# Recurrent layer and cross-attention: gates, scans and first scores set among earlier products

## The reference

```python
def rglru_scan(xc, w_a, b_a, w_x, b_x, lam, reverse):     # 16 blocks of 128 columns, two directions
    r = sigmoid(einsum('bshc,hce->bshe', xb, w_a) + b_a)
    i = sigmoid(einsum('bshc,hce->bshe', xb, w_x) + b_x)
    log_a = -RG_LRU_C * r * softplus(-lam)
    a = exp(log_a)
    u = sqrt(-expm1(2.0 * log_a)) * (i * xb)
    return scan of h = a * h + u along the 512 tokens

def rglru_layer(x, ...):
    h = rms_norm(x, norm_g)
    xr, gate = jnp.split(h @ w_in, 2, axis=-1)             # 2048 columns each
    xc = causal convolution of xr over 4 tokens
    y = rglru_scan(xc, ..., reverse=False) + rglru_scan(xc, ..., reverse=True)
    return x + (y * silu(gate)) @ w_out

# second block: mixer, then
x = x + merged @ w_out
def cross_attention(hn, memn, wq, wkv, wo):                # 256 memory rows, 4 heads of 256
    q = (hn @ wq).reshape(b, s, XA_HEADS, XA_DH)
    k, v = split(memn @ wkv)
    p = softmax(einsum('bshd,bmhd->bhsm', q, k) * XA_DH ** -0.5)
    return einsum('bhsm,bmhd->bshd', p, v).reshape(b, s, D_MODEL) @ wo
```

## Time and profile before

| | |
|---|---|
| median of 3 runs | 2404.89 us (2400.52 to 2405.05) |
| the profiled execution | 2402.92 us, of which the span is 2401.1 us |
| PE busy | 2277.0 us, 95% |
| PEld busy | 1807.1 us, 75% |
| DVE busy | 1503.6 us, 63% |
| ACT busy | 1269.8 us, 53% |
| POOL busy | 290.5 us, 12% |
| mean granted clock of PE | 0.98 |

### The profile page before, as it was taken

The page is one execution under the profiler, slowest core; times in us unless marked ns, Lnnn a source line. Parts: engine busy times, 40 slices in busy tenths (PEclk is TensorE's granted clock), DMA queues, the critical chain, the costliest instruction groups (busy, mean ns, idle before and its releaser), DMA issues. The chain is left out here.

```text
span 2401.1 us, 29505 instructions
## 1 busy us (share of the span) xinstructions
PE 2277.0 (95%) x11266; PEld 1807.1 (75%) x11266; DVE 1503.6 (63%) x1863; ACT 1269.8 (53%) x1677; POOL 290.5 (12%) x273
## 2 busy tenths in 40 slices
PE   7999899999998999999999999999996999999994
PEld 6878558877667768998888878888765777777773
DVE  4435742549996677666434545355237999888886
ACT  4334541468883445652324423225324988888884
POOL 2000000023330212240000000000000222212210
PEclk9999999999999999999999999999997999999997
DMA  7122103422224333001322312334224999999994
GB/s 238 62 70 90 51 1 111 129 88 88 88 66 162 129 111 119 19 1 36 105 88 88 106 36 72 127 117 158 71 81 168 400 409 411 407 401 402 399 401 184
DMA packets 119815, 377.39 MB, mean 157 GB/s; under 512 B 9608, under 2 KB 38592, under 8 KB 94496
## 3 DMA queue, kind: packets, MB, share of 16 engines
q1 hardware_dynamic: 106432, 332.49, 37.4%
q0 software_dynamic: 12768, 37.13, 4.7%
q10 hardware_dynamic: 512, 6.34, 0.7%
HBM read 363.02 MB, written 21.02 MB: 160 GB/s over the span
## 5 line engine op out<-in xcount | busy, mean ns | idle before, releaser
L2215 DVE TENSOR_TENSOR w_lo<-raw,w_hi 128x2048 fp32r<-128x2048 f32 x118 | 270.3, 2290 | 490.5 <-ACT w_hi L1570 490.4
L1570 ACT ACTIVATE w_hi<-raw 128x2048 fp32r<-128x2048 f32 x118 | 225.8, 1914 | 434.9 <-PE bank L848 385.8
L848 PE MATMUL bank<-hT_hi,w_hi 128*128 128x512 f32 x512 | 200.3, 391 | 3.7 <-DVE y_lo L2767 2.3
L848 PE MATMUL bank<-hT_lo,w_hi 128*128 128x512 f32 x512 | 199.7, 390 | 0.0
L848 PE MATMUL bank<-hT_hi,w_lo 128*128 128x512 f32 x512 | 199.7, 390 | 0.0
L1057 PE MATMUL bank<-hT_hi,w_hi 128*128 128x512 f32 x448 | 179.6, 401 | 1.8 <-DVE hT_lo L2279 1.8
L1057 PE MATMUL bank<-hT_hi,w_lo 128*128 128x512 f32 x448 | 174.6, 390 | 0.0
L1057 PE MATMUL bank<-hT_lo,w_hi 128*128 128x512 f32 x448 | 174.6, 390 | 0.0
L3006 DVE TENSOR_TENSOR e_lo<-eraw,e_hi 128x2048 fp32r<-128x2048 f32 x62 | 141.9, 2289 | 33.4 <-ACT e_hi L2102 33.4
L2890 DVE TENSOR_TENSOR e_lo<-raw,e_hi 128x2048 fp32r<-128x2048 f32 x64 | 146.4, 2288 | 12.0 <-ACT e_hi L2084 11.7
L2890 DVE TENSOR_TENSOR w_lo<-raw,w_hi 128x2048 fp32r<-128x2048 f32 x64 | 144.7, 2287 | 7.9 <-ACT w_hi L2084 7.6
(11 more groups left out here) (573 smaller groups left out, 5390.4 us busy)
## 6 DMA issues: line engine op xcount, KB each, us to landing
raw<-expert_w_gate SPq DMA_DIRECT2D x64, 1024.0 KB, 11.3
raw<-expert_w_up SPq DMA_DIRECT2D x64, 1024.0 KB, 11.6
eraw<-expert_w_down SPq DMA_DIRECT2D x64, 1024.0 KB, 10.7
raw<-w_in SPq DMA_DIRECT2D x40, 1024.0 KB, 5.1
raw<-even_w_in SPq DMA_DIRECT2D x18, 1024.0 KB, 5.2
raw<-odd_w_in SPq DMA_DIRECT2D x16, 1024.0 KB, 5.4
raw<-even_w_out SPq DMA_DIRECT2D x8, 1024.0 KB, 5.1
raw<-odd_w_out SPq DMA_DIRECT2D x8, 1024.0 KB, 5.1
```

Source lines behind the costliest of these rows:

```text
L848: mm = pe.matmul(out, st, mv, start=first and x == 0, stop=last and x == 2)
L1570: act.activation(w_hi[m % SPL][:], raw[n % RAW][:], ACT.Copy).then_inc(sem("hi_done"), 1)
L2215: dve.tensor_tensor(w_lo[m % SPL][:], raw[split_of[m] % RAW][:], f32(w_hi[m % SPL][:]), ALU.subtract).then_inc(sem("lo_done"), 1)
```

## The change

**Recurrent layer.** The gate products of the blocks 4s - 2 to 4s + 1 now stand behind the four tall panels of stage s (blocks 0 and 1 in stage 0), so only the groups 14 and 15 are left among the units of the output product. ACT's sigmoids, tables and silu, and DVE's `floors` and `recurrence`, have block numbers two higher at the same places of the stage, and fewer of them stand behind the last stage. There, `rnn_hi(0)` is followed by `gate_silu(7)`, and the splits of weights stand in other places.

The diff, with the context cut:

```diff
--- before.py
+++ after.py
@@ -1073,8 +1073,8 @@
                 tall((pn["xr"], pn["r_gate"])[q // 2][2 * s + q % 2], as_it_comes if s == 0 and q == 0 else hT)
-                if s:
-                    gates(4 * (s - 1) + q)
+                if s or q >= 2:
+                    gates(4 * s + q - 2)
         stage(wait=False)
@@ -1102,11 +1102,9 @@
 
-        gates(12)
         rnn_unit(0, 0)
-        gates(13)
+        gates(14)
         rnn_unit(0, 1)
-        gates(14)
         gates(15)
@@ -1367,8 +1365,10 @@
             return mg_hi[:, k], mg_lo[:, k]
-        gemm(pn["mix_out"], merged_in, False)
-        stage(wait=False)
+        gemm(pn["mix_out"][0:1], merged_in, False)
+        stage(wait=False)
+        banks_free(pn["mix_out"][1])
+        gemm_unit(pn["mix_out"][1], 0, merged_in, False)
         last = panels[pn["mix_out"][0]]
@@ -1377,19 +1377,22 @@
                     tr.then_inc(sem("norm_T"), 1)
+        gemm_unit(pn["mix_out"][1], 1, merged_in, False)
         pe.wait_ge(sem("norm_lo"), feat_at["mem"] + KD)
 ...
         gemm(pn["xv"], memT, False)
-        last = panels[pn["xv"][-1]]
-        pe.wait_ge(sem("evac_act"), last["at"] + last["nj"])
-        norm("x")
-        gemm(pn["xq"], hT_as_it_comes("x"), True)
-        stage(wait=False)
-        last = panels[pn["xq"][-1]]
-        pe.wait_ge(sem("evac_act"), last["at"] + last["nj"])
+        for half in range(2):
+            last = panels[pn["xv"][half]]
+            pe.wait_ge(sem("evac_act"), last["at"] + last["nj"])
+            for t in range(NT):
+                turn("x", t, range(4 * half, 4 * half + 4))
+        as_it_comes = hT_as_it_comes("x")
+        gemm(pn["xq"][0:1], as_it_comes, True)
+        banks_free(pn["xq"][1])
+        gemm_unit(pn["xq"][1], 0, hT, True)
         n_x = XH * NT
@@ -1397,7 +1400,7 @@
             for c in range(2):
-                mm = pe.matmul(psum[i % 4][:, 0:MEM], xqT[:, 2 * h + c, t * P:t * P + P], xkT[:, 2 * h + c],
+                mm = pe.matmul(psum[4 + i % 4][:, 0:MEM], xqT[:, 2 * h + c, t * P:t * P + P], xkT[:, 2 * h + c],
                                start=c == 0, stop=c == 1)
@@ -1407,26 +1410,45 @@
                 for m in range(MEM // P):
-                    mm = pe.matmul(psum[6 + c][:], xv[:, m, h * XD + c * P:h * XD + c * P + P], xpT[h % 2][:, m],
+                    mm = pe.matmul(psum[2 + c][:], xv[:, m, h * XD + c * P:h * XD + c * P + P], xpT[h % 2][:, m],
                                    start=m == 0, stop=m == MEM // P - 1)
 ...
 
+        heads_there = set()
+
+        def attended(k):
+            if k not in heads_there:
+                heads_there.add(k)
+                pe.wait_ge(*after("xa_lo", k + 1))
+            return xo_hi[:, k], xo_lo[:, k]
+
+        last = panels[pn["xq"][0]]
+        pe.wait_ge(sem("evac_act"), last["at"] + last["nj"])
         for i in range(3):
             xscores(i)
+        gemm_unit(pn["xq"][1], 1, hT, True)
+        stage(wait=False)
         for i in range(n_x):
 ...
                 xscores(i + 3)
+            if i == 0:
+                last = panels[pn["xq"][1]]
+                pe.wait_ge(sem("evac_act"), last["at"] + last["nj"])
             pe.wait_ge(*after("xa_norm", i + 1))
 ...
             for m in range(MEM // P):
-                tr = pe.transpose(psum[4 + i % 2][:, m * P:m * P + P], xprobs[i % 4][:, m * P:m * P + P], ident)
+                tr = pe.transpose(psum[i % 2][:, m * P:m * P + P], xprobs[i % 4][:, m * P:m * P + P], ident)
             tr.then_inc(sem("xa_tr"), 1)
 ...
                 xattend(i // NT - 1)
+            for j in {n_x - 3: (0, 1), n_x - 2: (2,), n_x - 1: (3,)}.get(i, ()):
+                pe.wait_ge(*after("xa_exp", n_x - 3 + j))
+                gemm_unit(pn["xo"][0], 0, attended, False, js=(j,))
         xattend(XH - 1)
-        stage()
-        gemm(pn["xo"], lambda k: (xo_hi[:, k], xo_lo[:, k]), False)
+        stage(wait=False)
+        gemm_unit(pn["xo"][0], 1, attended, False)
+        gemm(pn["xo"][1:2], attended, False)
         stage(wait=False)
@@ -1769,50 +1791,42 @@
                 gate_silu(2 * s - 1)
-            if s >= 2:
-                sigmoids(4 * s - 5)
-                tanhs(2 * s - 3)
-                exps(2 * s - 3)
+                sigmoids(4 * s - 3)
+                tanhs(2 * s - 2)
+                exps(2 * s - 2)
             conv_base(2 * s)
-            if s >= 2:
-                roots(2 * s - 3)
+            if s:
+                roots(2 * s - 2)
             hi_to(m + 3)
             if s:
-                sigmoids(4 * s - 4)
-            if s:
-                sigmoids(4 * s - 3)
+                sigmoids(4 * s - 2)
+                sigmoids(4 * s - 1)
             conv_base(2 * s + 1)
             if s:
-                tanhs(2 * s - 2)
+                tanhs(2 * s - 1)
             hi_to(m + 4)
             if s:
-                exps(2 * s - 2)
-                roots(2 * s - 2)
+                exps(2 * s - 1)
+                roots(2 * s - 1)
             gate_silu(2 * s)
             hi_to(m + 5)
-            if s:
-                sigmoids(4 * s - 2)
+            sigmoids(4 * s)
         stage(wait=False)
         rnn_hi(0)
+        gate_silu(7)
+        sigmoids(13)
+        hi_to(OUT0 + 2)
         rnn_hi(1)
-        gate_silu(7)
-        sigmoids(11)
-        tanhs(5)
-        exps(5)
-        hi_to(OUT0 + 2)
-        roots(5)
-        sigmoids(12)
-        sigmoids(13)
         tanhs(6)
+        hi_to(OUT0 + 3)
         exps(6)
-        hi_to(OUT0 + 3)
         roots(6)
 ...
         tanhs(7)
+        hi_to(OUT0 + 4)
         exps(7)
-        hi_to(OUT0 + 4)
         roots(7)
@@ -2044,8 +2058,8 @@
         norm_T("x", G_X, hT_hi)
-        gemm(pn["xq"], to(lambda x, j: xqT[:, 4 * x + j]))
-        stage()
+        gemm(pn["xq"][0:1], to(lambda x, j: xqT[:, j]))
+        act.activation(mark_a[0:1, 3:4], mark_a[0:1, 1:2], ACT.Exp)
         n_x = XH * NT
@@ -2053,24 +2067,29 @@
                 act.wait_ge(*after("xa_av", 2 * (h - 2) + 2))
-            act.activation(xpT[h % 2][:, :, t * P:t * P + P], psum[4 + i % 2][:, 0:MEM].rearrange("p (k s) -> p k s", s=P),
+            act.activation(xpT[h % 2][:, :, t * P:t * P + P], psum[i % 2][:, 0:MEM].rearrange("p (k s) -> p k s", s=P),
                            ACT.Copy).then_inc(sem("xa_pT"), 1)
 ...
                 act.wait_ge(*after("xa_av", 2 * h + c + 1))
-                act.activation(xo_hi[:, 2 * h + c], psum[6 + c][:], ACT.Copy).then_inc(sem("xa_hi"), 1)
+                act.activation(xo_hi[:, 2 * h + c], psum[2 + c][:], ACT.Copy).then_inc(sem("xa_hi"), 1)
 
 ...
                 act.wait_ge(*after("xa_tr", i - 3))
-            act.activation(xprobs[i % 4][:], psum[i % 4][:, 0:MEM], ACT.Exp, bias=col(T0 + i), scale=XD ** -0.5,
+            act.activation(xprobs[i % 4][:], psum[4 + i % 4][:, 0:MEM], ACT.Exp, bias=col(T0 + i), scale=XD ** -0.5,
                            accum_out=col(SUMS + i)).then_inc(sem("xa_exp"), 1)
+            if i == 2:
+                read(pn["xq"][1], 1, to(lambda x, j: xqT[:, 4 + j]))
+                stage(wait=False)
             if i >= 2:
 ...
                 xhead_hi(i // NT - 1)
+            if i in (4, 6):
+                hi_to(next_hi[0] + 1)
         xevac(n_x - 2)
@@ -2488,36 +2507,33 @@
             if s >= 2:
-                recurrence(4 * s - 7)
-                floors(2 * s - 3)
+                recurrence(4 * s - 5)
+            if s:
+                floors(2 * s - 2)
             conv(2 * s)
             lo_to(m + 3)
-            if s >= 2:
-                recurrence(4 * s - 6)
+            if s:
+                recurrence(4 * s - 4)
             conv(2 * s + 1)
 ...
             if s:
-                floors(2 * s - 2)
-            if s >= 2:
-                recurrence(4 * s - 5)
+                floors(2 * s - 1)
+                recurrence(4 * s - 3)
             lo_to(m + 5)
             if s:
-                recurrence(4 * s - 4)
+                recurrence(4 * s - 2)
         stage(wait=False)
         rnn_lo(0)
+        recurrence(11)
+        lo_to(OUT0 + 2)
         rnn_lo(1)
-        recurrence(9)
-        floors(5)
-        lo_to(OUT0 + 2)
-        recurrence(10)
         floors(6)
-        recurrence(11)
         lo_to(OUT0 + 3)
 ...
         recurrence(12)
-        floors(7)
         lo_to(OUT0 + 4)
         recurrence(13)
+        floors(7)
         lo_to(OUT0 + 5)
@@ -2847,27 +2863,26 @@
         dve.wait_ge(sem("h_back"), 16)
-        gemm(pn["mix_out"], add_to(resid), ahead=1)
-        stage(wait=False)
-        norm_T("mem", G_MEM, memT_hi, memT_lo, MEM // P)
+        gemm(pn["mix_out"], add_to(resid), ahead=1, before_last=lambda: norm_T("mem", G_MEM, memT_hi, memT_lo, MEM // P))
+        stage(wait=False)
         lo_to(next_lo[0] + 1)
 ...
         norm_T("x", G_X, hT_hi, hT_lo)
-        gemm(pn["xq"], None)
-        stage()
+        gemm(pn["xq"], None, ahead=0)
+        stage(wait=False)
         n_x = XH * NT
 ...
```

(8 more changed lines are left out.)

## The result

The changed kernel takes 2385.05 us (median of 4 runs, 2383.20 to 2387.88) against 2403.31: a ratio of 0.9926, 95% interval 0.9909 to 0.9943. It is 18.3 us faster; 12.2 were forecast. The profiled execution took 2384.67 us, 18.25 less than that of before. In three of the later series (the changed kernel again and the two with a moved loop split) one execution in twelve took 2410 to 2415 us; the medians hardly feel it, but the ratios of these three hold it and are some 0.001 high by it.

The account below looks back on a forecast made before the run. The product engine (PE), busy 95% of the span, was taken as the bound. Terms 5.4 + 3.3 + 0 + 5.2 - 1.7 = 12.2 us gave 2392.7 from the median 2404.9, stated as 2392; range 2386 to 2399.

Parts of the forecast that it names:

- rival 1: Whole kernel: new holes shorter than worked out and clock stays up; gain 17 to 18 us, 2387, chance 0.15.
- A: Recurrent layer: 10.6 us of holes and slow gates go, less new hole 3.5 and low clock 1.7; gain 5.4 us.
- B: Memory transposes: hole of 3.53 and 1.6 of low clock go, new key-product hole 1.8; gain 3.3 us.
- C: Transposes of the x norm: holes of 0.69 and 1.17 become one of 1.85 before the queries; gain 0.
- D: Cross-attention: 9.5 us out, less a score-loop hole of 2.6 and 1.7 of low clock; gain 5.2 us.
- the low clock's price for the new holes: Behind new holes in the recurrent layer and score loop, and one of the key or query holes: 1.7 us each.
- The 10.6 that go: Recurrent layer's gate products: holes of 4.86 and 2.43 us and slow gates of 1.5 and 1.8 disappear.
- Rivals 2 to 4: Loop splits stall PE twice, 2398, chance 0.17; VectorE bounds recurrent stages, 2410, 0.04; gain given back later, 2404, 0.02.

Follow-up runs that it names:

- the last kernel: Changed kernel with rp_lo early, key split between the row norms, loop split behind the first division, second query unit split behind the conversion of x: 2373.82 us (0.9887).
- cross-attention alone: Only the hunks of the transposes of x and of cross-attention, on the kernel before: 2393.56 us (0.9969).
- five more products: The changed kernel with five products more in the mixer's fifth panel, 1.1 us of work: 2388.78 us (0.9947).

## Why the prediction was wrong

**The whole.** The measured 2385.05 lies 7 us under the 2392 and 1 under the low end of the range. The gain is 6.1 us larger than forecast, and with its fourth run the kernel before has a median of 2403.3, 1.6 under the 2404.9 that the forecast started from. The direction and the places of the holes were right, and three of the four lengths. What came is nearest to rival 1 (2387, "the new holes are shorter than worked out and the clock stays up") in A, B and C; D came with the low clock, as forecast.

**The step that failed** is the low clock's price for the new holes. The prediction read 1.5 to 1.8 us behind holes of 2.4 us and more, and charged it (1.7) to the new holes of A and D and to one of those in B and C, 5.1 in all, as if the length decided. At these lengths (1.8 to 2.25) it does not. In the first profile 1.6 of the 5.1 came, in the second 4.7 (keys, queries and score loop). Over the ten profiles that have one or more of these holes, the clock never fell behind the first output product's (six profiles, 2.14 to 2.17 us), so the 1.7 in A was never paid; it fell behind the keys' 1.79 in five of seven, the queries' 2.08 in three of eight, the loop's 2.25 in three of five. For those three a chance of a half or so would have been the fair price.

Without any price the prediction's own sum gives 17.3 and 2387.6, still inside the range. What carried the time below it are the lower median of before (1.6), the shorter hole in A (1.3), the mixer (1.5) and 1.0 in the stretches that the table leaves out, less the 1.6 of low clock in D and the 1.55 that the router took back.

**A reading that was wrong** though its conclusion held: the eight small products behind the mixer's hole of 1.95 took 1.21 us, and the prediction took that as twice their normal time. The changed kernel's took 1.16 at full clock. The fall shows one row later, in the next sixteen products, before and after:

```profile
938.60 3.57 PE L1159 MATMUL bank<-nm 128*128 128x128 f32 x16
...
929.95 1.95 PE L1157 MATMUL bank<-nm 128*128 128x128 f32 x16
```

**A**, 8.50 against 5.4. The 10.6 that go were right for the profile they were read from, and 9.7 in the next one of the same kernel (holes of 4.86 and 1.72, slow gates 3.0 and 0.1). The 1.7 of low clock did not come. The hole was 2.16, not 3.5: PE came 0.7 us later than worked out (counted from the same start), since the gate group takes 3.6 us until it is out of the way and the prediction counted 3.0, and VectorE was 0.8 earlier. It shifted by 6.0 instead of 6.8: rp_lo starts at 660.52, where it started at 654.95 before, and the recurrent layer of the changed trace starts 0.45 sooner. The cause of that was not tried; ScalarE, whose split VectorE follows there, had a wait of 0.74 us for POOL at 627.81 before, which the changed kernel has not. The low clock and the hole make 5.4 + 1.7 + 1.3 = 8.4 of the 8.50.

**The mixer**, 1.49 against 0. The prediction took what lies behind the change as merely shifted. It was shifted, and that was the point: the same hole of 1.95 came at another time and kept its clock. The trace before alone could not tell: in it the clock fell behind each of the four holes of 1.95 to 2.43 us between 20 and 1810 us, the final norm's apart, and only a second execution shows that it need not. A term of plus or minus 1.7 for each hole of about 2 us downstream was missing in the range.

**B**: hole 1.79 as forecast, 3.20 in the first profile with the clock up, 1.7 to 1.8 in those where it fell; alone, the part's time cannot be told from nothing. **C**: 0, as forecast, with 27.51 to 27.53 for the stretch in all profiles but the last kernel's: the queries wait for the weight split ahead of hT_lo, and only moving that split (25.21) gave something. **D**: 5.95 against 5.2, with a hole of 2.25 for 2.6; the split at i = 4 is the cause, as forecast. The clock price there was right in this profile, and absent in that of cross-attention alone and that with five more products.

**The router** gave 1.55 back: the same hole of 1.30 us lay ahead, and in both the clock fell while PE was busy with the 64 light products of the router (36 columns each), but 2.8 us into them in the changed kernel's first profile and 4.8 us in that of before, so that they took 11.33 us instead of 9.47. That varied between executions too, from 2.8 to 6.0 us over all profiles; in the seven later profiles with the whole change the stretch was 19.4 five times, and 20.3 and 20.5.

Rivals 2 to 4 did not come: the recurrent stages kept their length, and nothing was lost in the experts.

## What to carry to other kernels

Where one engine is the bound, the place of the holes, and in three of four cases here their length to some tenths of a microsecond, can be read by following each releaser's queue through the new order. Then ask of each hole that is left which call stands on the releasing engine ahead of the one that is needed. Four such calls, moved into idle time, were worth another 11 us. A program's order is not its time: the split behind the third division was held up 10.7 us by a look-ahead that stood in front of it.

For holes of about 2 us, price the clock as a chance and not as a rule, and widen the range for every such hole downstream of a shift, touched or not. Take a second profile of the kernel before ahead of a forecast: a hole that is slow in one and fast in the other shows the chance. To compare two versions, compare stretches between the same instructions, over more than one profile of each; where a stretch with the same code moved, look at its granted clock first.

## What the runs showed of the hardware that was not expected

All counts are of the fourteen profiles. The holes of 4.86, 3.54 and 3.68 us that the change takes away occur fifteen times, and the clock fell at or behind fourteen of them (the 3.68 in the run of the recurrent part alone had 1.00 in the six microseconds behind it). Behind those of 1.30, 1.37 and 1.48 it stayed at 1.00 for at least five microseconds. Between, at 1.7 to 2.3 us, it went both ways: behind the untouched 2.06 at 283 us it fell in six profiles of fourteen, and behind the keys' 1.79 both in the same program (1.00 and 0.57). With a shift of 1.1 to 1.9 us it turned over (the mixer's 1.94: 1.00 and 0.65), and in the mixer the outcome follows the time since the clock's last rise without an exception. Why that time matters was not looked into further.

The price of one fall is not fixed either. The eight gate products behind the hole of 4.86 us, 3.59 us at full clock, took 5.11 and 5.31 us in two profiles and 6.62 to 6.73 in the other three.
